# A conditioned mixer with a mixture of experts on one core: input sections alternate between two raw places, modulation weights come in halves through three others

## The reference, cut to what matters

```python
mod = silu(c) @ w_ada + b_ada              # six vectors of 1024: sh_m, sc_m, g_m, sh_f, sc_f, g_f
h = rms_norm(x) * (1 + sc_m) + sh_m        # x: 256 tokens x 1024
z = h @ w_in                               # columns: sc_x | sc_B | sc_C | u | v | gate_A | gate_B
y_a = sc_B * causal_dwconv3(sc_C * sc_x)
v = layer_norm(gelu(v)) * ln_v_g
y_b = gelu(u) * (tril(w_spatial) @ v + b_spatial)      # per chunk of 128 tokens, 8 groups
x = x + g_m * ((sigmoid(gate_A) * y_a + sigmoid(gate_B) * y_b) @ w_out)
h = rms_norm(x) * (1 + sc_f) + sh_f
x = x + g_f * moe(h)                       # 32 experts, top 4 of each token, clamped SwiGLU
out = rms_norm(x)
```

## Time and profile before

| what | value |
|---|---|
| median of 3 runs | 1155.37 us (1152.95 to 1156.95) |
| the profiled execution's own time | 1153.63 us |
| its span | 1151.8 us |
| mean granted clock of TensorE | 0.953 |
| PE, DVE, ACT, POOL busy | 957.4, 357.2, 243.4, 8.6 us |
| moved | 467.30 MB, mean 406 GB/s |
| share of SP's queue in DMA time | 98.1% |

### The profile page before, as it was taken

How to read it: one execution, slowest core, us unless ns; L and a number is a source line. 1 busy time by engine, 2 the same in 40 slices (tenths; PEclk the granted TensorE clock), 3 DMA queues, 4 the chain that set the end, 5 groups by cost and what they waited for, 6 DMA issues and landing times.

```text
span 1151.8 us, 23787 instructions
## 1 busy us (share of the span) xinstructions
PE 957.4 (83%) x9707; PEld 505.7 (44%) x9708; DVE 357.2 (31%) x801; ACT 243.4 (21%) x365; POOL 8.6 (1%) x28
## 2 busy tenths in 40 slices
PE   7989999998986976987888888888876876876784
PEld 5789999743442321433333333443321322331331
DVE  3689796571221111212121121221211211211112
ACT  3435444530110110111111111110100100100112
POOL 0010000000000000000000000000000000000000
PEclk9989999999998998999998999999998998898997
DMA  9999788999999999999999999999999999999996
GB/s 358 377 340 357 293 311 318 412 400 428 427 425 427 426 426 427 426 426 425 425 426 427 427 426 426 427 426 427 426 426 426 427 426 427 427 426 426 427 424 273
DMA packets 62413, 467.30 MB, mean 406 GB/s; under 512 B 5180, under 2 KB 6516, under 8 KB 27572
## 3 DMA queue, kind: packets, MB, share of 16 engines
q1 hardware_dynamic: 62144, 466.65, 98.1%
q10 hardware_dynamic: 244, 0.29, 0.1%
HBM read 465.87 MB, written 1.05 MB: 405 GB/s over the span
## 4 chain that ended last, share of the span: by engine, by line
PE 42%; DMA 40%; SPq 8%; DVE 6%; issue 4%; ACT 1%; PEldq 0%; DVEq 0%; ACTq 0%
PE B L1405 22%; DMA trio<-in_w_down_dram 21%; DMA W<-in_w_down_dram 14%; PE B L1093 10%; SPq L411 4%; PE B L1424 3%; DMA W<-in_w_gate_up_dram 3%; SPq L413 3%; PE B L1414 2%; DVE wl L743 2%; DMA spare<-in_w_ada_dram 2%; PE B L1351 2%; PE B L1357 1%; DMA raw<-in_w_in_dram 1%; DVE spare L793 1%
## 5 line engine op out<-in xcount | busy, mean ns | idle before, releaser
L1405 PE MATMUL B<-W,trio 128*32 128x512 f32 (+1 forms) x4784 | 451.4, 522 | 85.6 <-DMA W<-in_w_gate_up_dram 77.3
L1405 PEld LDWEIGHTS B<-W,trio 128*32 128x32 f32 x4784 | 163.3, 112 | 347.7 <-issue 168.2
L661 ACT ACTIVATE EW<-EW 128x256 f32<-128x256 f32 x46 | 19.2, 416 | 683.1 <-DVE EW L1023 683.1
L1023 DVE TENSOR_SCALAR EW<-B 128x256 f32<-128x256 f32 x46 | 19.5, 425 | 463.9 <-PE B L1405 463.9
L1093 PE MATMUL B<-hh,wh 128*128 128x256 f32 x384 | 110.4, 288 | 4.2 <-DVE wl L743 4.2
L1093 PE MATMUL B<-hl,wh 128*128 128x256 f32 x384 | 109.8, 286 | 0.0
L1093 PE MATMUL B<-hh,wl 128*128 128x256 f32 x384 | 109.7, 286 | 0.0
L1414 PE MATMUL B<-b_gu,trio 128*32 128x512 f32 x368 | 50.4, 616 | 66.6 <-issue 55.2
L743 DVE TENSOR_TENSOR wl<-raw,wh 128x2048 fp32r<-128x2048 f32 (+1 forms) x36 | 73.3, 2074 | 18.2 <-ACT wh L556 17.7
L556 ACT ACTIVATE wh<-raw 128x2048 fp32r<-128x2048 f32 (+1 forms) x36 | 60.2, 1719 | 84.0 <-DMA raw<-in_w_in_dram 53.8
L1093 PEld LDWEIGHTS B<-hh,wh 128*128 128x128 f32 x384 | 74.9, 195 | 4.6 <-issue 4.0
(11 more groups left out here) (245 smaller groups left out, 689.8 us busy)
## 6 DMA issues: line engine op xcount, KB each, us to landing
W<-in_w_gate_up_dram SPq DMA_DIRECT2D x112, 2048.0 KB, 35.2
W<-in_w_down_dram SPq DMA_DIRECT2D x48, 2048.0 KB, 38.4
spare<-in_w_gate_up_dram SPq DMA_DIRECT2D x16, 2048.0 KB, 28.6
trio<-in_w_down_dram SPq DMA_DIRECT2D x15, 2048.0 KB, 41.0
raw<-in_w_in_dram SPq DMA_DIRECT2D x12, 2048.0 KB, 9.5
raw<-in_w_ada_dram SPq DMA_DIRECT2D x9, 2048.0 KB, 9.6
raw<-in_w_in_dram SPq DMA_DIRECT2D x4, 1024.0 KB, 15.7
raw<-in_w_out_dram SPq DMA_DIRECT2D x2, 2048.0 KB, 8.9
```

Of the source, the lines that this page charges most:

```text
L661: A(sg, gs, ACT.Sigmoid, scale=ALPHA).then_inc(sig_ready, 1)
L1023: V.tensor_scalar(halves(gs), paired(GU[:, 0:QC]), LIMIT, None, ALU.min).then_inc(gmin_ready, 1)
L1405: t = M(o, src[:, k % KQ, CAP * (k // KQ):CAP * (k // KQ) + CAP], w, start=(first and k == 0), stop=(k == KT - 1))
```

## The change

- **Places.** Sections use only two places of `raw`, in turn; a section is asked for when the section two before it has been split (`tenant_of`). The eight later units of `w_ada` leave the list. They come as sixteen halves of 1 MB through three half places: the two halves of `raw`'s third place and the second half of `spare`. A table (`HALVES_AFTER`) says behind which section SP asks for which halves; half c waits until half c - 3 has been weighed.
- **Weighing.** A table (`WEIGHED_IN`) puts the eight `weigh` steps into `SC_C`, `SC_B`, `GATE_A`, `U_`, `GATE_B` of h = 0 and `SC_C`, `SC_B`, `GATE_A` of h = 1. `sum_weighed(1)` moves behind product `U_` of h = 0; `sum_weighed(2)` stays behind `GATE_A` of h = 1. `add_bias(1)` moves behind `GATE_B` of h = 0.
- **ln_v_g.** It comes as 8 columns with the other small rows (one more transfer of ACT's queue, 64 rows instead of 56 in the first transpose, one more small copy of DVE) and is applied in the U step, where one tensor_tensor of 512 columns becomes two scalar_tensor_tensor of 256. The two multiplications L813 and the 512 KB load L389 are gone.
- **Small loads.** `w_spatial` is asked for behind `SC_B` instead of `SC_X`, `b_spatial` and the rest of `b_ada` behind `U_`, the router's and experts' small tables behind `SC_B` of h = 1.
- **Expert units.** Units 0 and 1 are asked for together after `ada_summed` 2, before the last `w_out` unit.

```diff
+    WEIGHED_IN = [(0, SC_C), (0, SC_B), (0, GATE_A), (0, U_), (0, GATE_B), (1, SC_C), (1, SC_B), (1, GATE_A)]
+    HALVES_AFTER = {(0, SC_C): (0, 1, 2), (0, GATE_A): (3, 4), (0, GATE_B): (5, 6), (1, SC_C): (7, 8), (1, SC_X): (9, 10),
+                    (1, SC_B): (11, 12), (1, GATE_A): (13, 14), (1, GATE_B): (15,)}
+    ADA_SUMMED = {(0, U_): 1, (1, GATE_A): 2}
+    BIAS_ADDED = {(0, GATE_B): 1, (1, U_): 2}
...
         def place(n):
-            return n if n < ASIDE[0] else n - len(ASIDE)
+            if n <= ASIDE[0]:
+                return n
+            return (split_units.index(n) + 1) % 2
...
+        ada_half_at = [raw[:, 2 * UW:2 * UW + UW // 2], raw[:, 2 * UW + UW // 2:3 * UW], spare[:, UW // 2:UW]]
...
+                if n == NU - 1:
+                    sp.wait_ge(ada_summed, NH)
+                    load(0, 0)
+                    load(1, 0)
...
+                if kind == "in" and s != V_:
+                    for c in HALVES_AFTER.get((h, s), ()):
+                        i, q, k = 1 + c // 8, c // 2 % 4, c % 2
+                        if c >= 3:
+                            sp.wait_ge(ada_half, c - 2)
...
+                        sp.dma_start(ada_half_at[c % 3], ada_v[q, :, k, 4 * HALF * i:4 * HALF * (i + 1)]).then_inc(s_ada[c % 3], 16)
...
             for a in range(TA):
-                step(V.tensor_scalar(HV[:, a, :], HV[:, a, :], stat[:, NMU + a:NMU + a + 1],
-                                     stat[:, VRST + a:VRST + a + 1], ALU.add, ALU.mult))
-                V.tensor_tensor(HV[:, a, :], HV[:, a, :], lng, ALU.mult).then_inc(v_ready, 1)
+                V.tensor_scalar(HV[:, a, :], HV[:, a, :], stat[:, NMU + a:NMU + a + 1],
+                                stat[:, VRST + a:VRST + a + 1], ALU.add, ALU.mult).then_inc(v_ready, 1)
...
-                        if b == 0 and n < 3:
-                            weigh(1 + h, n + 1)
-                        if b == 0 and s == GATE_B and h + 1 < NH:
-                            weigh(2 + h, 0)
+                        if b == 0 and (h, s) in ADA_WEIGHED:
+                            weigh(*ADA_WEIGHED[h, s])
...
-                    if s == GATE_A:
-                        sum_weighed(1 + h)
+                    if (h, s) in ADA_SUMMED:
+                        sum_weighed(ADA_SUMMED[h, s])
```

More of the change, by code:

```diff
@@ L140, in hybrid_trunk @@
         scm = late[:, 7 * P + 2 * E + 2 * KT:7 * P + 2 * E + 3 * KT]
+        lng = late[:, 7 * P + 2 * E + 3 * KT:7 * P + 2 * E + 4 * KT]
         sig = late[:, 8 * P:8 * P + HALF]
@@ L144, in hybrid_trunk @@
         hf = tmp[:, D:3 * D].rearrange("p (k t) -> p k t", t=T)
-        rows = EW[0:7 * KT, HALF:HALF + P]
+        rows = EW[0:8 * KT, HALF:HALF + P]
         row_sum = stat[:, 58:59]
@@ L186, in hybrid_trunk @@
         UNITS = 6
-        PLACE = ("spare", 2, 0, 8, 9, 1, 3, 4, 5, 6, 7, "trio")
+        PLACE = ("spare", 2, 1, 8, 9, 0, 3, 4, 5, 6, 7, "trio")
         TURN = 2
@@ L313, in place, with turn_of, tenant_of @@
         def place(n):
-            return n if n < ASIDE[0] else n - len(ASIDE)
+            if n <= ASIDE[0]:
+                return n
+            return (split_units.index(n) + 1) % 2
+        def turn_of(n):
+            return sum(1 for o in range(n) if o not in ASIDE and place(o) == place(n))
+        def tenant_of(n):
+            return max((o for o in range(n) if o not in ASIDE and place(o) == place(n)), default=None)
+        ada_half_at = [raw[:, 2 * UW:2 * UW + UW // 2], raw[:, 2 * UW + UW // 2:3 * UW], spare[:, UW // 2:UW]]
         def raw_slot(n):
@@ L318, in raw_slot @@
                 return aside_at[ASIDE.index(n)]
-            return raw[:, (place(n) % RING) * UW:(place(n) % RING + 1) * UW]
+            return raw[:, place(n) * UW:(place(n) + 1) * UW]
         def landed(n):
@@ L323, in landed @@
                 return s_aside[ASIDE.index(n)], 16
-            return s_slot[place(n) % RING], 16 * (place(n) // RING + 1)
+            return s_slot[place(n)], 16 * (turn_of(n) + 1)
         def product_done(eng, j):
@@ L355, in _, with load @@
             sp.dma_start(x_sb[:, :, :], x_in[0].rearrange("(a p) n -> p a n", p=P)).then_inc(s_x, 16)
-            for n, (kind, s, h) in enumerate(units):
-                if n not in ASIDE and place(n) >= RING:
-                    m = next(o for o in range(n) if o not in ASIDE and place(o) == place(n) - RING)
+            def load(u, e):
+                j = u % UNITS
+                if j < NQ:
+                    sp.dma_start(unit_pair(u).rearrange("p g n -> p (g n)"), gu_v[e, j]).then_inc(s_unit[u % SLOTS], 16)
+                else:
+                    sp.dma_start(unit_pair(u), dn_v[e, j - NQ]).then_inc(s_unit[u % SLOTS], 16)
+            for n, (kind, s, h) in enumerate(units):
+                m = None if n in ASIDE else tenant_of(n)
+                if n == NU - 1:
+                    sp.wait_ge(ada_summed, NH)
+                    load(0, 0)
+                    load(1, 0)
+                if m is not None:
                     if m in ada_units:
@@ L405, in _ @@
                         sp.dma_start(b_dn[E * i:E * i + E, :], b_down[0][:, h_dn * HALF:(h_dn + 1) * HALF]).then_inc(s_bdn, 16)
[L407 to L419, removed]
+            assert (place(NU - 2), place(NU - 1)) == (PLACE[2], PLACE[5]) and PLACE[1] == RING - 1
             sp.wait_ge(split_l, pieces_before[-2])
@@ L536, in _ @@
             act.dma_start(rows[5 * KT:7 * KT, :], b_ada[0][0:2 * D].rearrange("(k p) -> k p", p=P)).then_inc(s_rows, 16)
+            act.dma_start(rows[7 * KT:8 * KT, :], ln_v_g[0].rearrange("(k p) -> k p", p=P)).then_inc(s_rows, 16)
             act.wait_ge(cols_ready, 1)
@@ L718, in _ @@
             V.tensor_copy(cols[:, :], B[6][:, 0:7 * KT]).then_inc(cols_ready, 1)
+            step(V.tensor_copy(lng, B[6][:, 7 * KT:8 * KT]))
             dve.wait_ge(cols_ready, 1)
@@ L782, in weigh @@
             def weigh(i, q):
-                n = unit_no[("ada", i, q)]
-                dve.wait_ge(*landed(n))
+                c = 8 * (i - 1) + 2 * q
                 if q == 0 and i > 1:
                     dve.wait_ge(ada_summed, i - 1)
[L788 to L794, removed]
+                for k in range(2):
+                    w = ada_half_at[(c + k) % 3].rearrange("p (j n) -> p j n", j=4)
+                    dve.wait_ge(s_ada[(c + k) % 3], 16 * ((c + k) // 3 + 1))
+                    if q + k == 0:
+                        V.tensor_scalar(weighed[:, :, :], w, cT[:, 0:1], None, ALU.mult).then_inc(ada_half, 1)
+                    else:
+                        V.scalar_tensor_tensor(weighed[:, :, :], w, cT[:, 2 * q + k:2 * q + k + 1], weighed[:, :, :], ALU.mult, ALU.add).then_inc(ada_half, 1)
+                    dve.wait_ge(ada_half, c + k + 1)
                 if q == 3:
@@ L798, in _ @@
             split_low(2)
-            weigh(1, 0)
             split_low(3)
@@ L860, in _ @@
                             c = 2 * h + b
+                            dve.wait_ge(s_bs, 16)
                             dve.wait_ge(sp_done, c + 1)
[L862 to L865, removed]
+                            for t in range(2):
+                                g = 4 * h + 2 * b + t
+                                ts = slice(T * t, T * t + T)
+                                V.scalar_tensor_tensor(stmp[:, ts].rearrange("p (a n) -> p a n", a=TA), B[6][:, ts].rearrange("p (a n) -> p a n", a=TA),
+                                                       lng[:, g:g + 1], bs_all[:, g, :].unsqueeze(1).broadcast_to([P, TA, P]),
+                                                       ALU.mult, ALU.add).then_inc(sp_used, 1)
+                            dve.wait_ge(sp_used, 2 * c + 2)
                             dve.wait_ge(sec_act, act_bank(h, s, b))
@@ L1103, in _ @@
             keep_warm(WARM_FIRST, B[5])
-            pe.wait_ge(s_rows, 64)
-            TR(B[6][:, 0:7 * KT], rows, ident[0:7 * KT, 0:7 * KT]).then_inc(rowsT_done, 1)
+            pe.wait_ge(s_rows, 80)
+            TR(B[6][:, 0:8 * KT], rows, ident[0:8 * KT, 0:8 * KT]).then_inc(rowsT_done, 1)
             def modulation(part, g):
```

33 lines of the change are left out of this document (15 added, 18 removed).

## The result

The median is 1160.45 us (1158.27 to 1163.23, 20 runs) against 1154.32 for the kernel before (1152.95 to 1158.61, 20 runs): 1.0049 times as long, interval 1.0041 to 1.0056, slower by more than a measurement can miss. The forecast was 1160.3, reckoned from 1155.37; as a difference it was +4.9, and +6.1 was measured. The profiled execution took 1159.72, its span is 1157.9; the mean granted clock is 0.953 as before.

A forecast was written before the change was run, and what follows sets the result against it. Behind about 200 us the weight stream bounds the kernel, its start set by TensorE's mixer work. Terms -1.0 + 2.9 + 3.0 = +4.9 us on the median 1155.37 gave 1160.3, range 1152.5 to 1164.5.

The forecast's parts named there:

- sum ends, at full clock, against 120.41: First sum on TensorE, before GATE_B of h = 0: ends at 119.4 instead of 120.41, a gain of 1.0 us.
- clock behind the first sum: TensorE after its 4.5 us wait at sum_weighed(1): clock falls as in the earlier 3.8 us wait, costing 2.9 us.
- wait at the second sum: TensorE at sum_weighed(2): VectorE plus ACT's piece need 26.0 against two sections' 23.0, so a 3.0 us wait.
- clock behind the second sum: TensorE after its wait at sum_weighed(2): no fall of the clock counted, bounds 0 and 2.9 us.
- unit 3: Expert load after the last section's product: asked for 3 to 7 us after 204.4, moving the end by +4.9.
- The front gains, the sum gives it back: Mixer, h = 0: shorter wait before SC_B, then 4.5 us wait at sum_weighed(1); net gain 1.0 us.
- `SC_X` as before: Front of the mixer: SC_X lands as before, ACT starting on it at 56.56; no difference taken.
- rival 3: SC_X lands early, shortening VectorE's chain and the first wait, so not slower: 1152.0 to 1157; chance 0.29.
- rival 1: Both sums' waits drop TensorE's clock, the second costing 2.9 more: +7.8 us, 1163.2; chance 0.19.
- Unit 3 starts the stream: Expert weight stream: dense from that load on, so TensorE's late or early mixer end reaches the end one for one.
- At nothing: Extra small transfer, 64-row transpose, halves and asking for expert units 0 and 1 together: all priced at no cost.
- rule set beside the sum: TensorE's clock: the cold restart is paid at every wait, so both sums pay, 2.9 us more than forecast.

The follow-up runs named there:

- b_again: The kernel before, unchanged, profiled once more: 1156.05 us, one run.
- e1: The changed kernel with sum_weighed(1) alone moved between bank 0 and bank 1 of product GATE_B of h = 0: 1154.26 us, 0.9998 of the kernel before.
- a_again: The changed kernel, unchanged, profiled once more: 1158.52 us, one run.
- e6: The changed kernel with the old order of asking, expert units 0 and 1 behind the second w_out unit: 1159.4 us, 1.0043 of the kernel before.
- e4: The changed kernel with weigh(1, 0) put back into VectorE's idle time before the remainders of SC_X of h = 0: 1156.92 us, 1.0015 of the kernel before.
- e3: The changed kernel with transposes into an unused bank ahead of both sums' waits, keeping TensorE at work: 1156.58 us, 1.0015 of the kernel before.
- e2: The changed kernel with both sums moved between banks, into GATE_B of h = 0 and U_ of h = 1: 1148.66 us, 0.9947 of the kernel before.
- e5: The changed kernel with both sums between banks, weigh(1, 0) before SC_X's remainders, unit 1 asked for once the last half is weighed: 1147.03 us, 0.9930 of the kernel before.

## Why the prediction was right

Its account, term by term, in the changed kernel's profile:

| term | forecast | measured |
|---|---|---|
| sum ends, at full clock, against 120.41 | -1.0 | 118.22 + 0.99: -1.2 |
| clock behind the first sum | +2.9 | 0.95 + 0.90: +1.85 |
| wait at the second sum | +3.0 | +3.23 |
| clock behind the second sum | 0 (to 2.9) | 0.72 + 0.84: +1.56 |
| unit 3 | +4.9 | +5.44; its row says +5.50 |

That 1160.3 was forecast and 1160.45 measured is luck in part: the sum was 1.2 too small, and the median of three runs that it was added to was 1.05 above that of the twenty. Within the sum, the two terms of the clock were off by -1.05 and +1.56 and so nearly cancelled. The first row also varies: 120.41, from which it is counted, is 121.70 in b_again, the same kernel.

- *The front gains, the sum gives it back.* Right: no wait before `SC_B`, clock 1.00 there, then 4.49 where 4.5 was reckoned. `weigh(1, 3)` ended at 118.0; 118.4 was forecast. e1 takes the sum away from this chain and gets back 6.2.
- *`SC_X` as before.* Half right, by luck. ACT began on it at 57.44, 0.9 later than in the earlier trace rows, so rival 3 falls; the late front is not the reason, for a_again has 57.68. But its remainders took 4.49 instead of 5.34:

```profile
57.44 3.72 ACT L578 ACTIVATE wh<-raw 128x2048 fp32r<-128x2048 f32 x2 [3.20 <-DMA raw<-in_w_in_dram]
```

```profile
59.38 4.49 DVE L766 TENSOR_TENSOR wl<-raw,wh 128x2048 fp32r<-128x2048 f32 x2 [6.10 <-ACT wh L578]
```

  They ended at 63.87, before at 63.91. `w_spatial` is asked for one section later, and so GpSimd's steps from its masking on (58.38 to 65.0 before) start at 64.81, behind these remainders instead of beside them. The remainders took 5.34 and 5.36 in the two profiles of the kernel before and 4.49 or 4.50 in all eight of the changed one's forms; no run moves GpSimd's steps alone. I had priced the later small loads at nothing; by these rows they paid for the later landing.
- *The clock at the first sum.* The term that was mis-sized: I took the 2.9 of the wait before `SC_B`. Behind the same wait of 4.5 it cost 1.85 here, 2.3 in a_again (0.95 in the sum, 1.39 in the products), 2.3 in e6 and 1.8 in e4. 0.28 of each is no matter of the clock: at 1.00 in e3 the sum takes 1.06 and the 288 matmuls 34.77. So the fall itself cost 1.5 to 2.1. Right in kind, too large by 0.8 to 1.4.
- *The clock at the second sum.* "I count no fall" held in a_again, e4 and e6 and failed in the profile of the change and in e1 (1.6 each: in the table 0.84 of 1.56 is the next 96 matmuls, 12.36 for 11.52, and 0.72 is spatial, 1.81 for the 1.09 that it takes in e3 at full clock): the same wait of 3.23 in all five. So rival 1's second fall and the forecast's "no fall" were both true, each in some executions. The forecast also misread one of the two waits that it leaned on, since windows of 2 us don't show how long a wait is: the one at 428 us, after which the clock stayed up, was 2.84 and not about 2, so it was nearly the 3.0 forecast here and longer than the one at 416 us, after which it fell. TensorE's timeline of the kernel before:

```profile
416.09 3.40 PE L1405 MATMUL B<-W,trio 128*32 128x512 f32 x16 [2.04 <-DMA W<-in_w_gate_up_dram]
...
430.92 1.93 PE L1405 MATMUL B<-trio 128*32 128x256 f32 x32 [2.84 <-DMA trio<-in_w_down_dram]
```

  Both falls of the profile of the change together are worth 3.2, by unit 3 in e3.
- *Unit 3 starts the stream.* Right: unit 12 follows it one for one, and e1 and e2 move the end by about what they move unit 3 (unit 3 by 6.06 and 10.9, the medians by 6.2 and 11.8, the profiled executions by 6.3 and 9.6). One sign was drawn too tight: the eighth slice does not stay as before, since unit 3 is asked for within it. 0.6 of the difference between the two profiles lies behind unit 12; the two profiles of the kernel before differ by 1.1 there too.
- *At nothing.* Units 0 and 1: shown by e6. The halves never held VectorE up: in the profile of the change no `weigh` waits for one. The row transfer on ACT's queue and the wider transpose: TensorE's first modulation product begins at 11.53 (before 11.47).

Of the rule set beside the sum, that the clock's cold restart is paid anew at each long wait (the Trainium skill, TensorE: Matmul & The Clock Gate, "HAM oscillation — how this bites in real kernels"), the trace agrees for the wait of 4.5, in all four profiles that have it; for the one of 3.23 it does in two of five.

## What to carry to other kernels

A short step of one engine that needs the end of another engine's chain should stand in the middle of work that doesn't depend on it, not at its border: moving one sum by half a product was worth 6.2 us at the first place and 5.6 at the second in the medians, 6.1 and 4.9 in the asking for unit 3. When a change relieves a wait early in a chain, follow that chain to its next meeting point before counting the gain; and price the wait and the clock that falls behind it apart: e3 took away the second and left the first.

## What the runs showed of the hardware

- Of five waits of exactly 3.23 us, behind the same two sections, two were followed by the lower clock and three not. The waits of 4.49 to 4.50 us were followed by it in all four profiles that have them, but not from the same moment: from 116 to 118 us, with TensorE still waiting, the granted clock was 1.00 in the profile of the change and 0.55 in that of a_again, which lost 0.5 more.
- At the front, behind TensorE's wait for the first `w_ada` unit, the clock fell in four of the ten profiles: from 8 to 18 us it was 0.83 in those of the change, e1, e4 and e5 and 1.00 in the others, a_again among them. That alone did not make the first section late (51.49 in e1, 51.54 in e4). It began at 52.98 and 53.10 in the change and e5, where the clock fell once more, to 0.67 and 0.75 from 22 to 24 us and 0.50 from 24 to 26. What tells these executions apart is open; that all four are of the changed kernel's forms says little with only two profiles of the kernel before.
- VectorE's instruction on 128x2 took 1.00 in e4 and ended at 65.61, within 0.03 of GpSimd's at 64.49 + 1.09 = 65.58; elsewhere it takes 0.17. The Trainium skill (SBUF — State Buffer, "Who interferes with whom") says that a tensor_scalar of VectorE, when it runs in a mode that uses two ports, and an instruction of GpSimd shut each other out of the ports that they share: the one that issues first holds them to its end. This row agrees; whether the instruction ran in that mode no trace shows. 0.8 us on VectorE's chain hung on when GpSimd began a step that nobody waits for.
